# Memory values computed with tokens on partitions, keys' tiles first; the third weight tile split in halves of k

## The reference, cut to what matters

```python
def memory_attention(q, mk, mv):
    s = jnp.einsum('bshd,bmhd->bhsm', q, mk).astype(jnp.float32) * (X_HEAD_DIM ** -0.5)
    p = jax.nn.softmax(s, axis=-1)
    o = jnp.einsum('bhsm,bmhd->bshd', p.astype(mv.dtype), mv)
    return o.reshape(B, S, X_Q)
...
        h = rms_norm(x, norm_mix_pre[l])
        z = h @ w_in[l]
...
        mkv = rms_norm(mem, norm_mem[l]) @ w_mem_kv[l]
        mk, mv = jnp.split(mkv, 2, axis=-1)
        ox = memory_attention(qx.reshape(B, S, X_HEADS, X_HEAD_DIM),
                              mk.reshape(B, N_MEM, X_HEADS, X_HEAD_DIM),
                              mv.reshape(B, N_MEM, X_HEADS, X_HEAD_DIM))
```

## Time and profile before

| | before |
|---|---|
| median of 3 runs | 803.94 us (803.89 to 804.21) |
| profiled execution, its time | 803.75 us |
| its span | 802.0 us |
| TensorE busy | 791.6 us, 99% of the span |
| VectorE busy | 455.7 us, 57% |
| ScalarE busy | 353.8 us, 44% |
| TensorE's share of the chain that ended last | 90% |

### The profile page before, as it was taken

How to read it: one execution, slowest core, us unless ns; L and a number is a source line. 1 busy time by engine, 2 the same in 40 slices (tenths; PEclk the granted TensorE clock), 3 DMA queues, 4 the chain that set the end, 5 groups by cost and what they waited for, 6 DMA issues and landing times.

```text
span 802.0 us, 11669 instructions
## 1 busy us (share of the span) xinstructions
PE 791.6 (99%) x4648; PEld 690.7 (86%) x4648; DVE 455.7 (57%) x550; ACT 353.8 (44%) x603; POOL 46.9 (6%) x99
## 2 busy tenths in 40 slices
PE   8999999999999999999999999999999999999997
PEld 8988778777777888888888999999999999888885
DVE  5743546566424523515655589888888887833222
ACT  5833545555446223324443455444444445632111
POOL 1100001144000000000001110000000000000000
PEclk9999999999999999999999999999999999999999
DMA  9831221312311333323471013333333344631011
GB/s 296 253 115 61 76 82 54 105 54 55 103 53 53 106 105 105 105 84 135 149 262 54 12 42 105 106 105 105 105 105 105 105 131 157 226 142 53 0 53 52
DMA packets 67925, 83.66 MB, mean 104 GB/s; under 512 B 3488, under 2 KB 61360, under 8 KB 67888
## 3 DMA queue, kind: packets, MB, share of 16 engines
q1 hardware_dynamic: 67712, 83.13, 31.8%
q10 hardware_dynamic: 176, 0.01, 0.0%
HBM read 81.02 MB, written 2.11 MB: 104 GB/s over the span
## 4 chain that ended last, share of the span: by engine, by line
PE 90%; DVE 4%; ACT 1%; DMA 1%; issue 1%; POOL 1%; SPq 0%; DVEq 0%; POOLq 0%; ACTq 0%
PE pair L1306 84%; PE pair L1423 1%; DMA raw<-in_w_mem_kv 1%; PE pair L1437 1%; PE pair L1404 1%; PE pair L1412 1%; PE pair L1442 1%; ACT probs L682 1%; POOL B_f L644 1%; DVE T_f L1193 1%; DVE op_lo L1173 1%; DVE T_lo L1200 0%; PE pair L1321 0%; PE pair L1338 0%; PE pair L1313 0%
## 5 line engine op out<-in xcount | busy, mean ns | idle before, releaser
L401 DVE TENSOR_TENSOR w_lo<-raw,w_hi 128x1024 fp32r<-128x1024 f32 x66 | 83.1, 1261 | 104.3 <-ACT w_hi L396 104.3
L1306 PE MATMUL pair<-hT_hi,w_hi 128*128 128x512 f32 x336 | 135.6, 403 | 0.0
L1306 PE MATMUL pair<-hT_hi,w_lo 128*128 128x512 f32 x336 | 131.2, 390 | 0.0
L1306 PE MATMUL pair<-hT_lo,w_hi 128*128 128x512 f32 x336 | 130.9, 390 | 0.0
L396 ACT ACTIVATE w_hi<-raw 128x1024 fp32r<-128x1024 f32 x66 | 69.6, 1056 | 97.6 <-PE pair L1306 81.0
L1306 PE MATMUL pair<-T_hi,op_hi 128*128 128x256 f32 x320 | 90.6, 283 | 0.5 <-DVE op_lo L1173 0.5
L1306 PE MATMUL pair<-T_lo,op_hi 128*128 128x256 f32 x320 | 90.6, 283 | 0.0
L1306 PE MATMUL pair<-T_hi,op_lo 128*128 128x256 f32 x320 | 90.6, 283 | 0.0
L1306 PEld LDWEIGHTS pair<-hT_hi,w_hi 128*128 128x128 f32 x336 | 63.1, 188 | 14.2 <-issue 1.0
L1306 PEld LDWEIGHTS pair<-hT_lo,w_hi 128*128 128x128 f32 x336 | 63.2, 188 | 13.4 <-issue 1.0
L1306 PEld LDWEIGHTS pair<-hT_hi,w_lo 128*128 128x128 f32 x336 | 63.1, 188 | 13.5
(11 more groups left out here) (191 smaller groups left out, 1553.2 us busy)
## 6 DMA issues: line engine op xcount, KB each, us to landing
raw<-in_w_in SPq DMA_DIRECT2D x42, 512.0 KB, 4.8
raw<-in_w_ffn_up SPq DMA_DIRECT2D x22, 512.0 KB, 4.8
raw<-in_w_ffn_gate SPq DMA_DIRECT2D x22, 512.0 KB, 4.2
raw<-in_w_ffn_down SPq DMA_DIRECT2D x22, 512.0 KB, 4.0
raw<-in_w_branch_a SPq DMA_DIRECT2D x8, 512.0 KB, 4.0
raw<-in_w_out SPq DMA_DIRECT2D x8, 512.0 KB, 3.7
raw<-in_w_mem_kv SPq DMA_DIRECT2D x6, 512.0 KB, 6.6
x_in<-in_x SPq DMA_DIRECT2D x4, 512.0 KB, 8.2
```

The lines of the kernel that those rows point to most:

```text
L401: eng.tensor_tensor(lo, raw_view(s), hi.bitcast(F32), ALU.subtract).then_inc(weights_split, 1)
L1306: ins = pe.matmul(dst, a, b, start=first and n == 0, stop=last and n == 2, skip_group_check=onto)
```

## The change

The order of the steps becomes `mem` 0 to 7, so keys first. The value tiles (steps 4 to 7) are computed with memory tokens as the stationary operand: one tile of PSUM now holds 128 tokens (the first or second half, m) on partitions by 256 channels of two heads. Such a tile reads the weights of two steps at once. To let one operand span two slots, the three slots become one tensor, `w_ring`. Steps 4 and 5 (and 6 and 7) both read the slots of the pair, and so `MV_FIRST` shifts the wait of `wait_split_free` by one tile for steps 7 and 9. Each tile still has 24 matmuls of 256 columns. The 8 transposes of the values go, the copies go to `mv_raw`, and VectorE scales `mv_raw` into `mv` after the copies of v. Step 2's tile is split in two halves of k: its first half has a semaphore of its own, `second_in`, and TensorE may start on k slices 0 to 3 when `half_split` is 3.

```diff
-    steps = [[("mem", h)] for h in (4, 5, 6, 7, 0, 1, 2, 3)]
+    steps = [[("mem", h)] for h in range(8)]
...
+    w_ring = sb("w_ring", narrow_at[0], [P, 3, 2, 8, P], F32R)
+    w_hi = [w_ring[:, i, 0, :, :] for i in range(3)] + [sb("w_hi3", narrow_at[3], [P, 8, P], F32R)]
...
-    mvT = sb("mvT", 176, [P, X_HEADS, N_MEM])
+    mv_raw = sb("mv_raw", 176, [P, MT, X_HEADS, P])
...
             if kind == "step" and n >= 3:
-                eng.wait_ge(tile_full, step_end[n - 3])
+                eng.wait_ge(tile_full, step_end[n - 3 + (n - 3 in MV_FIRST)])
...
-        E_MV, E_V = E_X + 2, E_X + 4
+        E_MV, E_V = E_X, E_X + 2
+        MV_FIRST = (4, 6)
...
-                    load_half(c, h, early_in if c == 2 else raw_in[c % 2])
+                    load_half(c, h, early_in if c == 2 else second_in if c == 1 and h == 0 else raw_in[c % 2])
...
-                    dst = mk[:, i, :] if i < X_HEADS else mvT[:, i - X_HEADS, :]
+                    c, m = divmod(i - X_HEADS, 2)
+                    dst = mk[:, i, :] if i < X_HEADS else mv_raw[:, m, 2 * c:2 * c + 2, :].rearrange("p h d -> p (h d)")
...
-            done = 2
+            act.wait_ge(second_in, 16)
+            act.activation(split_at(2)[0][:, 0:4, :], raw_view(2)[:, 0:4, :], ACT.Copy).then_inc(half_hi, 1)
+            act.wait_ge(raw_in[1], 16)
+            act.activation(split_at(2)[0][:, 4:8, :], raw_view(2)[:, 4:8, :], ACT.Copy).then_inc(weights_hi, 1)
+
+            done = 3
...
-            done = 2
+            hi, lo = split_at(2)
+            for ks, hi_done, n, signal in ((slice(0, 4), half_hi, 3, half_split), (slice(4, 8), weights_hi, 3, weights_split)):
+                dve.wait_ge(hi_done, n)
+                dve.tensor_tensor(lo[:, ks, :], raw_view(2)[:, ks, :], hi[:, ks, :].bitcast(F32), ALU.subtract)\
+                   .then_inc(signal, 1)
+
+            done = 3
...
+                    dve.wait_ge(tile_copied, copied_no[("mem", 7)])
+                    for m in range(MT):
+                        c = NORM_MEM + m
+                        dve.tensor_scalar(mv[:, m, :, :], mv_raw[:, m, :, :], rstd[:, c:c + 1], None, ALU.mult)\
+                           .then_inc(mv_ready, 1)
...
-                pe.wait_ge(weights_split, at_stream[("step", s)] + 1)
+                if s == 2:
+                    pe.wait_ge(half_split, 3)
+                else:
+                    pe.wait_ge(weights_split, at_stream[("step", s)] + 1)
+                if kind == "mem" and i >= X_HEADS:
+                    m = i % 2
+                    pe.wait_ge(weights_split, at_stream[("step", s - m)] + 2)
+                    slot = (s - m) % 3
+                    w = w_ring[:, slot:slot + 2, :, :, :]
+                    for k in range(KT):
+                        ins = three(dst[:, 0:2 * P], w[:, :, 0, k, :], w[:, :, 1, k, :],
+                                    memT_hi[:, k, P * m:P * m + P], memT_lo[:, k, P * m:P * m + P],
+                                    k == 0, k == KT - 1, swap=True)
+                    ins.then_inc(tile_full, 1)
+                    return
...
+                    if s == 2 and k == 4:
+                        pe.wait_ge(weights_split, 3)
...
+                    pe.wait_ge(mv_ready, MT)
...
-                    for m in range(MT):
-                        e = E_X + m
-                        pe.wait_ge(turned_split, e - 3)
-                        for h in range(X_HEADS):
-                            ins = pe.transpose(bk(4 + e % 4)[:, P * h:P * h + P], mvT[:, h, P * m:P * m + P], ident[:, :])
-                        ins.then_inc(rows_turned, 1)
```

More of the change, by code:

```diff
@@ L148, in encoder_block @@
     narrow_at = [16, 24, 32, 196]
-    w_hi = [sb(f"w_hi{i}", a, [P, 8, P], F32R) for i, a in enumerate(narrow_at)]
-    w_lo = [sb(f"w_lo{i}", a + 4, [P, 8, P], F32R) for i, a in enumerate(narrow_at)]
+    w_ring = sb("w_ring", narrow_at[0], [P, 3, 2, 8, P], F32R)
+    w_hi = [w_ring[:, i, 0, :, :] for i in range(3)] + [sb("w_hi3", narrow_at[3], [P, 8, P], F32R)]
+    w_lo = [w_ring[:, i, 1, :, :] for i in range(3)] + [sb("w_lo3", narrow_at[3] + 4, [P, 8, P], F32R)]
     hT_hi, hT_lo = sb("hT_hi", 40, [P, KT, SEQ], F32R), sb("hT_lo", 56, [P, KT, SEQ], F32R)
@@ L280, in encoder_block @@
         raw_in = [sem(f"raw_in{i}") for i in range(2)]
-        early_in = sem("early_in")
+        early_in, second_in = sem("early_in"), sem("second_in")
         mem_loaded = [sem(f"mem_loaded{i}") for i in range(2)]
@@ L299, in encoder_block @@
         probs_ready, probs_turned, probsT_ready = (sem(n) for n in ("probs_ready", "probs_turned", "probsT_ready"))
+        mv_ready = sem("mv_ready")
         o_full, o_hi_done, o_split = sem("o_full"), sem("o_hi_done"), sem("o_split")
@@ L386, in raw_count @@
         def raw_count(c):
-            return 32 * (c // 2 + 1) - (0 if c % 2 else 16 if c == 0 else 48)
+            return 32 * (c // 2 + 1) - (16 if c < 2 or c % 2 else 48)
         def split_hi(eng, s):
@@ L1119, in _ @@
                         dve.wait_ge(rows_turned, e + 1)
-                        if e < E_MV:
-                            c = NORM_MEM + e - E_X
-                            ins = dve.tensor_scalar(mv[:, e - E_X, :, :], as4(bk(4 + e % 4)), rstd[:, c:c + 1], None,
-                                                    ALU.mult)
-                        else:
-                            ins = dve.tensor_copy(v_c[:, 4 * (e - E_MV):4 * (e - E_MV) + 4, :], as4(bk(4 + e % 4)))
-                        ins.then_inc(turned_split, 1)
+                        dve.tensor_copy(v_c[:, 4 * (e - E_MV):4 * (e - E_MV) + 4, :], as4(bk(4 + e % 4)))\
+                           .then_inc(turned_split, 1)
+                    dve.wait_ge(tile_copied, copied_no[("mem", 7)])
[3 more added lines that the diff above has]
+                           .then_inc(mv_ready, 1)
             for t in steps[NS - 1]:
```

## The result

The changed kernel takes 814.26 us (median of 4 executions, 811.51 to 816.8), the kernel before 804.08 us beside it (803.89 to 804.64, 4 executions): a ratio of 1.0125, interval 1.0107 to 1.0143. The sign was forecast. The size was not: 811.4 us was forecast, and 814.26 lies above the range of 810.0 to 813.5. The changed kernel also scatters over 5.3 us, where the one before scatters over 0.75. Of its four executions, 811.51 us has a mean granted clock of 0.996, 812.82 has 0.994, 815.7 has 0.992 and 816.8 has 0.990.

The account below looks back on a forecast made before the run. TensorE, busy 791.6 of 802.0 us, was taken as the bound. Step 8's 8.28 us delay less 0.87 for transposes gave +7.41 on 803.75: 811.16, as a median 811.35 us; range 810.0 to 813.5.

Parts of the forecast that it names:

- Step 2 by halves: Step 2 follows step 1 without a hole, 0.65 us earlier, a gain that vanishes in the wait at step 4.
- Step 4 needs two tiles: Step 4 waits for the splits of steps 4 and 5, starting at 22.80 instead of 21.26 us: +1.54 us.
- Step 6's hole: Ahead of step 6, TensorE waits for step 7's split, whose slot tile 5 still reads: a 2.56 us hole.
- The second turns' hole: Between tile 7 and step 8, turned x waits behind step 9's split; step 8 starts 8.28 us late in all.
- x's last scaling: Scaling of x's last tile, delayed behind step 7's split to 33.4 us, stays hidden before the turns by 0.8 us.
- The transposes: Eight value transposes go at the end of step 10, a full gain of 0.87 us on TensorE.
- Two-block operands: Value matmuls streaming two blocks a slot apart cost nothing extra; rival: slower, up to 822.9 us, chance 4%.
- The clock: Whether TensorE's clock falls in the three new holes; forecast without it 811.4 us, with it 812.9 us or more.
- the first rival: TensorE's clock falls in a hole, 1.5 us lost: once gives 812.9 us, in all three 815.9; chance 12%.

Follow-up runs that it names:

- filled: Changed kernel with unread transposes on TensorE in the holes: 8 ahead of step 4, 24 ahead of step 6, 30 ahead of the second turns; 810.15 us.
- fourth_place: Changed kernel with step 7's split in an SBUF place of its own and step 9's in a slot free since step 5; 806.07 us.
- both_early: Kernel of `early_halves` with step 7's split done a round earlier, right behind step 6's; 803.17 us, ratio 0.9988.
- no_halves: Changed kernel with step 2's tile split in one piece again; 814.68 us, ratio 1.0132.
- turn_first: Changed kernel with ScalarE and VectorE taking turned x blocks 0 to 3 ahead of step 9's split in round 7; 809.58 us.
- early_halves: Kernel of `fourth_place` with the early chunk's two tiles (steps 4 and 5) split and used in halves of k; 803.66 us.
- fourth_filled: Kernel of `fourth_place` with 8 unread transposes on TensorE ahead of step 4; 804.68 us, ratio 1.0006.

## Why the prediction was wrong

- *Step 2 by halves*, 0.65 us that vanish at step 4: right. Alone it is worth 803.81 against 804.15 us, within the measurement, and taking it out changes nothing.
- *Step 4 needs two tiles*, start at 22.80: the size is off in some executions. It was 21.63 in one profile, 22.90 in the other. The chain is right; the landing of the early chunk was taken as 18.64 us, give or take 0.5, and its split starts at 17.3 in some profiles and at 18.6 to 18.9 in others.
- *Step 6's hole*, forecast as 2.56 us of delay, of which 2.40 idle: measured 2.72 (30.17 - 27.45) and 2.56, the same in both profiles, with the releasers named. The equal 2.56 is chance. The handovers were priced at 0.04 us each; here 0.10 us pass from TensorE's last matmul to the high part (27.61 to 27.71) and 0.14 from the low part to step 6 (30.03 to 30.17). The chain is right.
- *The second turns' hole*: the forecast had 3.1 us of idling, measured 3.16. Without falls step 8 starts 7.15 us late (`filled`); the forecast's 8.28 less the 1.17 of the landing gives 7.11.
- *x's last scaling*, hidden by 0.8 us: it ended at 32.15 us, ahead of the turns at 34.51. Right.
- *The transposes*, 0.87 us: right, by the starts of step 8 and the spans in `fourth_place`, `filled` and `both_early`.
- *Two-block operands*, priced at nothing: right. Step 7's 24 matmuls run from 36.17 to 39.01, 2.84 us for 23 distances, 0.12 each, and the same in `fourth_place` with blocks 96.5 KB apart.
- *The clock*: wrong, and more than the whole error, since the early landing gave 1.2 us back in some executions: 814.26 - 811.4 = 2.9 us were missing, and the falls cost up to 4.1 in the profiles. The step that failed is the judgement on the first rival, that "these holes are short, and lie in steady work", and its 12%. The rows behind it were holes of up to 0.7 us, and say nothing of 2 to 3 us; the nearest row for a long wait was the start at half pace, which spoke for the rival. The price given to it was right: 1.5 us for a fall, measured 1.3 to 1.46. But the forecast treated three holes as one question with two answers; in nine executions at least one fell each time, by times and clocks. Two falls with the early landing give 812.8 us, three with the late one 815.45; the median of 814.26 is the middle between an execution of the one kind and one of the other (812.82 and 815.7).

The trace here agrees with the Trainium skill (TensorE: Matmul & The Clock Gate, "HAM oscillation"), which says that waits between groups of matmuls can bring the throttled clock back: of the ten holes of over 2 us in the profiled executions of the changed kernel (two profiles), `no_halves`, `turn_first` and `fourth_place`, eight have the slower pace behind them, and filler work keeps the granted clock at 1.00.

## What to carry to other kernels

When an operand comes to span two slots of a ring, every release is one tile later, and everything placed behind that split on each engine waits too: move independent work ahead of it, or give the late tile a place of its own. A wait of 2.3 to 3.2 us in dense TensorE work costs its length and, in a share of the executions, 1.3 to 1.5 us more for the clock, so price each hole with both and look at whether the runs fall into groups. If a hole can't be closed, work without a reader in it gives the second part back.

## What the runs showed of the hardware that was not expected

- Idle times of 2.3 to 3.2 us let the granted clock fall from 1.00 to 0.50 in eight of ten holes (all three of 3.16 us, five of the seven of 2.3 to 2.6), some of them only after TensorE had started again. The holes of 0.98, 1.12, 1.39 and 1.63 us in the profiles of the changed kernel, `early_halves`, `fourth_filled` and `no_halves` show none. Whether such a short one can do it is open: `early_halves` was 2.5 us slower in 3 of 12 executions, two of them at a clock of 0.996 but the third, 806.32 us, at 0.998 like the fast ones, and no trace of these shows how long their holes were.
- The clock column can't be trusted at the start: 1.00 at half pace, where behind these holes it says 0.50.
- The same transfer lands at about 17.3 or 18.6 us in executions of one program, 10.4 or 11.7 us after its issue, and the 1.2 us move through the whole chain. Why it does so is open.
- Open: the slowest executions, 816.4 to 816.8 us, lie 1.0 to 1.4 us above the 815.45 that three falls (4.1 us) and the late landing (1.2) add to 810.15. Their mean granted clock is 0.990. It was 0.996 in the profile with one fall (`no_halves`), 0.994 and 0.995 in those with two, 0.992 in the one with three. So the means point to one fall more, which at 1.35 us would be about the difference. No trace of such an execution was taken, so where it would lie is not shown.
